# A compressor layer over the sample rows: fp32 products become three fp32r products, with its buffers, turns and queues laid out anew

## What is computed

```python
hid = jax.nn.silu(jnp.einsum('nilgd,ldf->nigf', blocks + pos_emb[None, None, :, None, :],
                             w1.reshape(CMP_LEN, hd, CMP_HIDDEN)))
return jnp.einsum('nigf,fd->nigd', hid, w2)
```

## Time and profile before

| | us |
|---|---|
| median of 3 runs | 1924.54 (1919.97 to 1925.21) |
| the profiled execution | 1926.79 |
| its span, first to last instruction | 1924.6 |
| PE busy | 1855.1 (96%) |
| DVE, ACT, POOL busy | 860.2, 694.2, 389.0 |
| the samples' phase: first turn to last product with values | 988.7 to 1355.3 |
| mean granted clock of PE | 0.98 |

### The profile page before, as it was taken

How to read it: one execution, slowest core, us unless ns; L and a number is a source line. 1 busy time by engine, 2 the same in 40 slices (tenths; PEclk the granted TensorE clock), 3 DMA queues, 4 the chain that set the end, 5 groups by cost and what they waited for, 6 DMA issues and landing times. The chain is left out here.

```text
span 1924.6 us, 35242 instructions
## 1 busy us (share of the span) xinstructions
PE 1855.1 (96%) x13566; PEld 1451.6 (75%) x13566; DVE 860.2 (45%) x2578; ACT 694.2 (36%) x1529; POOL 389.0 (20%) x553
## 2 busy tenths in 40 slices
PE   7999999998998999999999999999899999999898
PEld 6777777687866988788885555554688888888797
DVE  5222222686555353122411121212677787877534
ACT  5100000564433141010003323322577777777422
POOL 0000000002650000000022112110355556655100
PEclk9999999998997999999999999999899999999899
DMA  5434443565788563744345143241400000000463
GB/s 209 167 133 144 150 145 114 178 192 156 254 272 277 188 219 115 252 153 148 87 181 195 45 154 102 97 115 53 127 22 20 24 24 24 13 8 13 169 208 137
DMA packets 158532, 254.06 MB, mean 132 GB/s; under 512 B 33858, under 2 KB 109824, under 8 KB 154016
## 3 DMA queue, kind: packets, MB, share of 16 engines
q1 hardware_dynamic: 143904, 205.99, 33.0%
q0 software_dynamic: 4608, 33.56, 4.9%
q10 hardware_dynamic: 9856, 12.26, 2.1%
HBM read 205.85 MB, written 52.96 MB: 134 GB/s over the span
## 5 line engine op out<-in xcount | busy, mean ns | idle before, releaser
L1818 POOL TENSOR_SCALAR sparse_pr<-sparse_pr,sparse_coef,sparse_gate 128x63 f32<-128x63 f32 (+8 forms) x384 | 245.8, 658 | 183.7 <-DVE sparse_coef L1770 183.7
L1115 PE MATMUL x_acc<-x_w_hi,x_y_lo 128*128 128x478 f32 (+3 forms) x768 | 275.8, 359 | 2.3 <-DVE x_y_lo L963 2.2
L1115 PE MATMUL x_acc<-x_w_lo,x_y_hi 128*128 128x478 f32 (+3 forms) x768 | 270.1, 352 | 0.0
L1115 PE MATMUL x_acc<-x_w_hi,x_y_hi 128*128 128x478 f32 (+3 forms) x768 | 269.6, 351 | 0.0
L2971 PE MATMUL ss_ps_h<-ss_xT,cmp_w 128*128 128x508 f32 x512 | 244.0, 594 | 0.8 <-ACT ss_xT L2812 0.8
L1709 ACT ACTIVATE sparse_pr<-sparse_pr,sparse_nmax 128x63 f32<-128x63 f32 (+8 forms) x384 | 227.2, 598 | 1.1 <-DVE sparse_nmax L1764 1.1
L489 PE MATMUL h_acc<-h_w_hi,h_y_lo 128*128 128x512 f32 x448 | 177.5, 396 | 0.8 <-DVE h_y_lo L414 0.8
L489 PE MATMUL h_acc<-h_w_hi,h_y_hi 128*128 128x512 f32 x448 | 174.8, 390 | 0.0
L489 PE MATMUL h_acc<-h_w_lo,h_y_hi 128*128 128x512 f32 x448 | 174.6, 390 | 0.0
L1115 PEld LDWEIGHTS x_acc<-x_w_hi,x_y_lo 128*128 128x128 f32 x768 | 146.5, 191 | 28.9 <-issue 14.7
L1115 PEld LDWEIGHTS x_acc<-x_w_hi,x_y_hi 128*128 128x128 f32 x768 | 146.3, 190 | 11.4
(11 more groups left out here) (387 smaller groups left out, 2653.4 us busy)
## 6 DMA issues: line engine op xcount, KB each, us to landing
h<-cmp_w SPq DMA_DIRECT2D x56, 256.0 KB, 2.1
h_w_side<-in_even_w_in SPq DMA_DIRECT2D x16, 896.0 KB, 5.1
h_w_raw<-in_even_w_in SPq DMA_DIRECT2D x6, 2048.0 KB, 8.1
x_w_side<-in_odd_w_in SPq DMA_DIRECT2D x16, 716.0 KB, 4.8
cmp_lent<-in_odd_w_in SPq DMA_DIRECT2D x5, 1912.0 KB, 8.7
h<-x_out SPq DMA_DIRECT2D x40, 239.0 KB, 2.5
ev_unit<-in_cache_a_k SPq DMA_DIRECT2D x4, 2048.0 KB, 9.1
ev_unit<-in_cache_a_v SPq DMA_DIRECT2D x4, 2048.0 KB, 12.1
```

Source lines behind the costliest of these rows:

```text
L1115: last = nc.tensor.matmul(acc[b][:, 0:passes[p][3]], left[:, k, t * P:(t + 1) * P], weights(right, p)[:, k, :], start=(k == 0 and a == 0), ...
L1818: nc.gpsimd.tensor_scalar(row, row, one, gate[:, t, 2 * i + e, (br + 1) % 3:(br + 1) % 3 + 1], ALU.mult, ALU.mult).then_inc(scaled, 1)
```

## The change

It changes the samples' phase, and the memory that it shares with its neighbours:

- The first layer's weights are cut at the phase's start: ACT casts `w1` to `w_hi` (four casts of 2048 columns), DVE subtracts for keys and POOL for values (`w_lo`, two subtractions of 2048 columns each).
- One turn now takes one row position `l` for both samples and heads (512 columns). ACT casts the bank to `x_hi`, DVE subtracts to `x_lo` (rings of 5), and both halves of the hidden layer are computed for this `l` and `l` + 8 before the next: 6 fp32r products of 512 columns in each of 32 half steps `hh` of a pair. The turn for a position is made three positions ahead (`AHEAD`), through the boundary of units too.
- `scores`, `down_k` and the compressed scores move to half steps 1 to 4 of the values. The turns of `psel` 2 and 3, `pwin` and `pnew` move into the next pair's keys.
- POOL scales `psel` in two parts and copies pieces in halves; one buffer serves selected keys and then selected values of a pair, so keys are gathered after the pair before has used its values.
- Window rows, their turns and `pselT` live in the memory of `w1`, so their first loads wait for the cuts. SP issues the loads of new rows ahead of a pair's output stores. Some later buffers swap places (`SparseLoads`, `OutLoads`).

```diff
+    TURNS_K = {0: [("psel", 2), ("psel", 3)], 1: [("pwin", 0)], 2: [("pnew", 0)], 5: [("win", 0)], 6: [("win", 1)]}
+    TURNS_V = {6: [("pc", 0)], 15: [("psel", 0), ("psel", 1)]}
+    for q in range(6):
+        TURNS_K.setdefault(10 + q, []).append(("ks", q))
+    TURNS_K[15].append(("new", 0))
+    for q in range(6, 8):
+        TURNS_V.setdefault(q - 6, []).append(("ks", q))
...
+        if hh % 2 == 0:
+            n = (2 * p + m) * KD + hh // 2 + AHEAD
+            if n < N_STEPS:
+                turns.append(("x", n // (2 * KD), n % (2 * KD)))
...
+                    for s in range(2):
+                        lw = KD * s + l
+                        for i, (w, x) in enumerate(((w_hi, x_lo), (w_lo, x_hi), (w_hi, x_hi))):
+                            ins = nc.tensor.matmul(ps_h[c][:, :], w[m][:, lw, c * P:(c + 1) * P], x[b][:, s:s + XW],
+                                                   start=l == 0 and s == 0 and i == 0, stop=l == KD - 1 and s == 1 and i == 2)
...
+            nc.scalar.copy(x_hi[n % N_X][:, 0:XW], ps_t[nb][:, :]).then_inc(x_high, 1)
...
+            nc.vector.tensor_tensor(x_lo[n % N_X][:, 0:XW], ps_t[nb][:, :], x_hi[n % N_X][:, 0:XW].bitcast(F32), ALU.subtract
+                                    ).then_inc(bank_free[nb], 1)
...
-                    nc.gpsimd.tensor_scalar(psel[:, :], psel[:, :], coef[:, 1:2], gate[:, p, 1:2], ALU.mult, ALU.mult).then_inc(scaled, 1)
+                    for part in (slice(0, 1024), slice(1024, NKEY)):
+                        nc.gpsimd.tensor_scalar(psel[:, part], psel[:, part], coef[:, 1:2], gate[:, p, 1:2], ALU.mult, ALU.mult).then_inc(scaled, 1)
...
+                        load_new(sp, p + 1)
+                        load_rows(sp, p + 1, vw_in, wins[1], vw_loaded)
                         following.store_pair(sp, p)
-                        load_rows(sp, p + 1, vw_in, wins[1], vw_loaded)
-                        load_new(sp, p + 1)
```

More of the change, by code:

```diff
@@ L3060, in _ @@
                         comp.hidden(m, xT_p[m], NCB, ps_h[m], c).then_inc(p_hidden, 1)
+                    if m == 1:
+                        for n in range(AHEAD):
+                            turn("x", 0, n)
                 pe.wait_ge(q_loaded, 32)
@@ L3122, in _ @@
                                              ACT.Silu, bias=comp.bias[:, m, c:c + 1]).then_inc(p_active, 1)
[L3123 to L3124 removed]
+                for n in range(AHEAD):
+                    take_x_high(act, 0, n)
                 act.wait_ge(gate_in, 16)
@@ L3151, in _ @@
-                    for slot in range(HS):
-                        for what, x in TURNS_V.get(slot, ()):
-                            if what == "kc":
-                                if p + 1 < PAIRS:
-                                    take(act, what, p + 1, x)
-                            elif by_act(what, x):
-                                take(act, what, p, x)
-                        if slot == 17:
-                            silu(1, p, 0)
+                    for hh in range(HALVES):
+                        takes(0, p, hh)
+                        if p and hh == 1:
+                            take_v(p - 1)
+                        if hh >= HALVES - 2:
+                            silu(0, p, hh - HALVES + 2)
@@ L3262, in _ @@
                     nc.vector.tensor_reduce(nmax[:, 1:2], mins[:, 0:5], AX, ALU.min).then_inc(sel_max, 1)
-                    dve.wait_ge(sel_probs, p + 1)
-                    dve.wait_ge(win_probs, p + 1)
-                    nc.vector.reciprocal(coef[:, 1:3], lsum[:, 1:3]).then_inc(coef_ready, 1)
-                    for what, x in (("psel", 1), ("psel", 3), ("pnew", 0)):
+                nc.vector.memset(q_all[:, :, :], 0.0).then_inc(q_zero, 1)
+                for b in range(N_X):
+                    nc.vector.memset(x_lo[b][:, XW:XW + 2].bitcast(F32), 0.0)
+                    last = nc.vector.memset(x_hi[b][:, XW:XW + 2].bitcast(F32), 0.0)
@@ new lines, in _ @@
+                for n in range(AHEAD):
+                    take_x_low(dve, 0, n)
+                dve.wait_ge(q_zero, 1)
+                dve.wait_ge(turned, turned_after("q", 0, 0))
+                to = q_all[:, :, :].rearrange("p n (g j r) -> p n g j r", g=2, r=8)
+                nb, nu = bank("q", 0, 0)
+                for g in range(2):
+                    half = slice(g * HD, (g + 1) * HD)
+                    src = ps_t[nb][half, 0:256].rearrange("p (r n j) -> p n j r", r=8, n=NB)
+                    last = nc.vector.tensor_scalar(to[half, :, g, :, :], src, -SCALE, None, ALU.mult)
@@ L3267, in _ @@
+                for what, p, x in LAST_TURNS:
+                    if not by_act(what, x):
                         take(dve, what, p, x)
```

498 lines of the change are left out of this document (279 added, 219 removed).

## The result

| | before | after |
|---|---|---|
| median of the runs, us | 1924.11 (4 runs, 1919.97 to 1925.21) | 1891.84 (4 runs, 1890.4 to 1893.86) |
| ratio | | 0.9833, 95% interval 0.982 to 0.9846 |
| profiled span | 1924.6 | 1888.6 |

The change makes the kernel 32 us faster; 1889 was forecast, with a range of 1879 to 1904. To see where the time went I cut both traces at the same four points of the samples' phase: first product of the prompt, first product of the samples, start of the last such product, end of the last product with values.

A forecast was written before the change was run, and what follows sets the result against it. PE, busy 96% of the span, was taken as the bound. Products -44.4, start -2.5, moved turns +2.2, waits +8.9, end -0.9 make -36.7 us against 1924.6; with 1.2 us added, 1889 us, range 1879 to 1904.

The forecast's parts named there:

- A, the products: Samples' first layer: 768 fp32r products at 0.2266 us, 174.0 us, replace 218.4 us of fp32 products; gain 44.4 us.
- The turns' pitch: Turns between fp32r products in the samples' loop: 1.2 us added for their pitch, which no row shows, and for gathers.
- B, the start: Samples' phase start: first product at about 1015.0 instead of 1017.50 us, gain 2.5; five turns go into the loop, loss 2.2.
- C, new waits: Samples' loop: PE newly waits for banks, copies, scaling and silu, 2.35 us a pair; loss 8.9 us in all.
- `psel` 0 for the scaling: Behind half step 15 of the values: PE wants POOL's first scaled part at +10.84, ready +11.2; wait 0.4 us a pair.
- silu at the pair's boundary: Between pairs: silu of the values' half 0 ends at +12.25, PE wants to go on at +12.1; wait 0.25 us.
- D, gathers: Selected keys, gathered behind `times_v`, land in time with some 2 us to spare; cost 0, up to 3 us a pair.
- SP's order: Loads of rows ahead of 16 stores: whatever the order costs is hidden, as the rows are wanted half a pair later.
- E, the end: Samples' phase end: 12.0 us from the last product's end plus 1.6 for the clock, against 11.4; gain 0.9 us after corrections.
- a slower odd column: Rival, chance 0.05: fp32r products reading x from an odd first column stream slower; at half pace +87 us, 1976.
- the clock did fall: Rival, chance 0.06: waits between pairs make PE's clock fall, 1.6 us twice a pair; +13 us, 1902.
- more waits than counted: Rival, chance 0.20: turns behind a position wait another 0.3 us each, gathers add 1 us a pair; 13.6 us, 1902.

The follow-up runs named there:

- d1_fp32: Changed kernel with one fp32 product in place of three fp32r ones, low parts cut but not multiplied: 1928.79 us, ratio 1.0011 to the kernel before.
- c1_even: Changed kernel with all products reading x from column 0, so half of the positions use wrong columns: 1890.47 us, phase 327.01.
- c2_wide: Changed kernel with the row length of the ten ring buffers of x changed from 514 to 528 numbers: 1891.83 us, phase 328.74.
- f1_fixed: Changed kernel with all 768 products using the same 128 weight columns and the high part of x from column 0: 1886.78 us, one execution, phase 326.85.
- c3_psel: Changed kernel with the turn of psel 2 moved behind half step 15 of the values, DVE copying the even ones: 1888.30 us, phase 325.09.
- d4_pc: Changed kernel with the compressed probabilities' turn ahead of the position's turn in half step 6 of the values: 1891.08 us, phase 327.68.
- e2_whole: Changed kernel with POOL's scaling of psel undivided: 1895.06 us, phase 329.72.
- d2_two: Changed kernel with one product of the three left out (w_lo by x_hi): 1851.05 us, phase 288.18.
- e3_stores: Changed kernel with SP's order as before, a pair's 16 stores ahead of the loads of window values and new rows: 1891.25 us, phase 328.64.
- c0_changed: The changed kernel run again, unedited: 1891.48 us, ratio 0.9826 to the kernel before, phase 329.08.
- d3_start: Changed kernel with the first three turned positions moved up among the prompt's products: 1889.99 us, phase 327.60.
- e1_all: Changed kernel with the edits of c3_psel, d4_pc and d3_start together: 1883.92 us, ratio 0.9792 to the kernel before, phase 321.26.

## Why the prediction was right

**A, the products: right in kind, mis-sized by 5.7 us.** The prediction took 0.2266 us a product from the earlier trace rows; the loop runs at 0.232 and 0.236, mean 0.234: 768 x 0.234 = 179.7 us, not 174.0, and the gain is 38.7 us where 44.4 stood. d1_fp32 confirms the size from the other side: with fp32 products the phase is 37.0 us longer, where 256 x 0.86 - 179.7 gives 40.5. Of the 3.5 us between, 2.5 are waits that shrink there (share product and silu; the waits of the loop are 4.4 us by starts, where the changed kernel has 7.0); the rest I did not take apart. The odd first column is 1.5 us of the miss (c1_even); the other 4 stay unexplained: not the buffers' place (c2_wide), not the weights (f1_fixed), not the work beside. The prediction also gave two reasons why 174.0 us stand where four passes against three would give 163.8. The first, 512 columns for 508, makes 165.1. For the second, that a short product pays its own start, no run shows the 8.9 us that are left.

**The turns' pitch: 1.2 us was allowed, and the turns themselves cost nothing new.** A product behind a turn starts 0.36 us after it, 0.08 earlier than 0.44, but the product after that comes 0.087 us late. A single turn between products thus takes 0.45 us more than the stream without it, before and after alike. What is left of the loop's miss when pace, clock and waits are taken off says that all work between the products cost 0.9 us more than counted; this is a difference, not a reading.

**B, the start: right.** 3.05 us against 2.5. The third turn, held up by the two banks, starts 18.2 us behind the prompt's first product, where the forecast had 18.9. Not foreseen was that the clock would fall behind its wait: six products in 2.70 us (1011.90 to 1014.60) instead of 1.50 as in c3_psel, 1.2 us that the loop's row above pays. The weights' cuts are hidden. DVE's two took 4.48 us (forecast 4.8). POOL's two took more than twice its copy of 1.89 us, 4.5 us each, and were done at 1011.5 instead of 1010, for use at 1045:

```profile
993.56 2.79 POOL L2813 COPY ss_pieces<-ss_c_in 128x1024 f32<-128x1024 f32 x1 [3.16 <-DMA ss_c_in<-in_cache_c_kcmp,cmp_rows]
...
1002.54 9.00 POOL L2923 TENSOR_TENSOR ss_w_lo<-cmp_w,ss_w_hi 128x2048 fp32r<-128x2048 f32 x2
```

**C, new waits: 7.0 us in the loop where 8.25 stood** (8.9 less the 0.65 that falls behind the last pair). By the steps, counted from starts as in the forecast:

| wait | forecast | measured | |
|---|---|---|---|
| `psel` 3 for the position's bank, a pair | 1.2 | 1.13 | held 2.0 us from the turn's start, 0.88 between; shown to be order alone by c3_psel |
| share product, a pair | 0.5 | 0.24 | wanted at 1142.13 us, starts at 1142.37; gone in d4_pc |
| `psel` 0 for the scaling, a pair | 0.4 | 0 | see below |
| silu at the pair's boundary | 0.25 | 0.63 | gone when another turn stands there (c3_psel) |
| silu of the first pair's keys, once | 0.7 | 0.73 | product at 1043.83 us |

The step that failed is `psel` 0. Counted from the sum product (1144.54 us), the scaling starts at +9.54 (forecast 9.95), and its first part is done at +10.75 (11.2), although it takes 1.2 us and not 1.03. PE asks for it at +11.41 (10.84), because 7 half steps take 10.2 us, not 9.5: the pace is slower, and the second product behind each turn is late. So 0.66 us are to spare where 0.4 were missing.

But the gain is lost one step later. The silu was to end at +12.25 and ends at +12.77. The table load before it is held up by the cast of a position, and that cast by its turn, which the slower products have put off too:

```profile
1154.73 0.59 ACT L2863 CAST ss_x_hi<-ss_ps_t 128x512 fp32r<-128x512 f32 x1 [1.56 <-PE ss_ps_t L2966]
1155.34 1.28 ACT L3165 ACT_TABLE_LOAD   x1
1156.63 0.68 ACT L3165 ACTIVATE ss_hid<-ss_ps_h,cmp_bias 128x508 f32<-128x508 f32 x1
```

PE would have opened the next pair at +12.20 (forecast 12.1, with the wait for `psel` 0 in it) and does so at +12.83. The two waits of the boundary together are 0.63 us where 0.65 stood: the sum is right, its parts are not, and that is luck. It is also why undividing the scaling costs 0.6 us and not 4 (e2_whole): the whole is done 0.5 us late, and the silu would have been waited for anyway. What the two parts buy here is almost nothing; they would buy more if the products were shorter (in d2_two PE idles 2.7 us a pair behind the first part alone).

**D, gathers: right.** No wait on a transfer in the loop; the first gather of selected keys is issued at 1099.31 us and its rows are turned at 1109.70. Nor is there one in d2_two, where they are wanted sooner. **SP's order: right** (e3_stores).

**E, the end: mis-sized by 2 us.** Its forecast had 1.6 us for a fallen clock, as in the earlier trace rows. The idle times are now 0.24 and 0.55 us, where the kernel before had 1.60 and one of 0.55 behind it, and the clock stayed at 1.00:

```profile
1309.71 1.20 PE L2990 MATMUL ss_ps_t<-constants_shared,ss_psel 128*128 128x128 f32 x8 [0.24 <-ACT cmp_w L2850]
...
1314.35 3.71 PE L3089 MATMUL ss_ps_o<-ss_ks_in,cmp_w 128*64 128x128 f32 x64 [0.55 <-ACT cmp_w L3173]
...
1319.45 0.44 PE L3100 MATMUL ss_ps_o<-cmp_w,ss_pcT 127*64 127x128 f32 x4
```

**The total was nearer than its parts.** In the loop and the end: pace +5.7, clock at the start +1.2, waits in the loop -1.3, work between the products -0.3 (the difference of above), end -2.2; with the start, -0.5, this is the measured miss of 2.6 us in the phase. Forecast terms that were too low by 6.9 us met others that were too high by 4.3. Of the rivals, a slower odd column exists, but at 1/25 of the size that would have decided; the clock did fall, but once, at the start, not between pairs, where PE idles 0.38 and 0.96 us; "more waits than counted" went the other way.

## What to carry over

- When the engine that bounds a loop changes its kind of work, take its new pace from the nearest row, but leave a per cent or three for it: 3% of the pace was the largest error here, larger than any wait.
- Waits of a bank that two turns in a row cause are paid only for the order in which the turns stand. Spread them, let one fill a wait that is there anyway, and let the copy of a turn go to the engine whose queue is free: 1.25 us a pair for two lines of a table and one of the choice of engine.
- Read a wait as the distance of two starts, less what that distance is without a wait. The idle time of the profile leaves out the draining before it: 0.38 us stood where 0.63 were lost.
- A margin counted against a bounding engine grows when that engine turns out slower and shrinks when it gets faster. In d2_two, with a third of the products gone, the chain from the sum product to POOL's scaling was the largest wait, 10.7 us of idle time.

## What the runs showed of the hardware

**The clock at the phase's start.** Thirteen executions with the new layout are compared at 1000 to 1020 us. Eleven have the same instructions there, with PE idle for 1.04 us before the third turn. In seven of them (the first, c0_changed, c1_even, c2_wide, d1_fp32, d4_pc, e2_whole) the clock then fell to 0.50 and the way from the prompt's first product to the samples' first took 21.3 to 21.4 us. In four (c3_psel, d2_two, e3_stores, f1_fixed) it stayed at 1.00, and this way took 21.9 to 22.1 us, because the prompt's products had run at half clock for longer. In e3_stores, in windows of 2 us at the place where the changed kernel's stood at 0.50 and 0.86, it is 1.00, and start and loop together take 316.95 us against 317.38. The loop alone gains 1.0 us where the clock stays up, and the longer half clock at the start takes 0.6 back: the two courses differ by 0.4 us net. An idle time of 1 us is thus not enough to say whether the clock falls. The eleven differ in when the clock had risen: 2.5 to 3.6 us behind the prompt's first product in the seven, 5.3 to 5.8 in the four. Why that should decide, no run shows. Where the idle time was taken away the clock stayed up both times, but in d3_start it had risen at 5.4 us, as in the four that need no help; only e1_all, at 3.0 us, speaks for the edit. That is one execution.

**POOL and DVE held up each other.** In the rows under B, POOL's copy of 1024 columns that starts at 993.56 us takes 2.79 us; the other 31 of its kind take about 1.04. DVE subtracts from 990.97 to 995.45 us with both operands in SBUF, and the copy ends 0.9 us after that. In ten of the thirteen traces of the new layout the copy begins during DVE's second subtraction, takes 1.64 to 3.18 us, and ends 0.90 us after DVE each time. In the other three (c2_wide, d4_pc, e3_stores) it begins during the first, ends 0.90 us after that one, and now DVE pays: its second subtraction takes 3.1 us instead of 2.28. The two subtractions of c2_wide take 5.32 us together, where the changed kernel's take 4.48:

```profile
991.50 5.32 DVE L3325 TENSOR_TENSOR ss_w_lo<-cmp_w,ss_w_hi 128x2048 fp32r<-128x2048 f32 x2
...
993.52 1.16 POOL L2813 COPY ss_pieces<-ss_c_in 128x1024 f32<-128x1024 f32 x1 [2.67 <-DMA ss_c_in<-in_cache_c_kcmp,cmp_rows]
```

So whichever came second stood still until the other was about done (the copy's 0.90 us behind DVE are 0.14 less than it takes alone). The Trainium skill says so in "SBUF — State Buffer", section "SBUF: two separate sides": a DVE operation with two SBUF inputs and a GpSimd operation that reads SBUF share a port pair, and whichever begins second is blocked entirely. All thirteen traces agree with it. In the changed kernel it cost nothing, since the tile beside it landed only at 997.

**Behind a turn.** The distance from the first fp32r product behind an fp32 turn to the second is 0.319 us (65 places), behind other fp32 work 0.341 (30), not 0.232. That is some 9 us over the loop. Behind a turn it is paid back by the shorter distance from the turn to the product, 0.36 us instead of 0.44: a single turn costs the stream 0.45 us in both kernels.
